# A decoder layer on one core: prompt compression moved under the GLA normalisation, sample constants made earlier, and another order of branches and page loads for the last four samples

## The reference

```python
def compress(kv, w1, b1, w2, pe):            # prompt and samples, keys and values alike
    ...
    first = jnp.einsum('bnpgd,pdh->bngh', ch + pe[:CMP_STRIDE, None, :], w1r[:CMP_STRIDE])
    second = jnp.einsum('bnpgd,pdh->bngh', ch + pe[CMP_STRIDE:, None, :], w1r[CMP_STRIDE:])
    hid = jax.nn.gelu(first[:, :-1] + second[:, 1:] + b1)
    return jnp.einsum('bngh,hd->bngd', hid, w2)

o_gla = rmsnorm(o_gla.astype(x.dtype), gla_norm_g) * jax.nn.silu(...)      # the normalisation
o_nsa = gates[:, :, 0] * o_cmp + gates[:, :, 1] * o_slc + gates[:, :, 2] * o_win
```

## Time and profile before

| | |
|---|---|
| median of 3 runs | 2411.33 us (2409.88 to 2413.12) |
| the profiled execution | 2411.11 us, its span 2409.5 us |
| busy in the span | PE 2166.9 us (90%), PEld 1748.8 (73%), DVE 883.5 (37%), ACT 435.9 (18%), POOL 487.8 (20%) |
| mean granted clock of TensorE | 0.953 of full speed |
| GLA | 429 to 545 us |
| compression | 546 to 582 us |
| samples | 582 to 700 us |
| prompt's attention | from 700 us |

### The profile page before, as it was taken

The page is one execution under the profiler, slowest core; times in us unless marked ns, Lnnn a source line. Parts: engine busy times, 40 slices in busy tenths (PEclk is TensorE's granted clock), DMA queues, the critical chain, the costliest instruction groups (busy, mean ns, idle before and its releaser), DMA issues. The chain is left out here.

```text
span 2409.5 us, 30785 instructions
## 1 busy us (share of the span) xinstructions
PE 2166.9 (90%) x11874; PEld 1748.8 (73%) x11874; DVE 883.5 (37%) x1520; ACT 435.9 (18%) x897; POOL 487.8 (20%) x425
## 2 busy tenths in 40 slices
PE   3789999887669888999999998799999999999994
PEld 3678888666346555788888665588888888888883
DVE  1443122662236656521121114622232222534336
ACT  0241000331125555200000012311111000000001
POOL 2112210003011111522121122622322223000002
PEclk9899999895879999999999999899999999999997
DMA  8432112636320000101211210311111111122421
GB/s 238 118 94 80 38 35 65 175 81 166 103 73 1 1 1 1 36 25 45 48 31 44 81 35 27 107 35 50 37 35 52 35 52 35 48 87 93 151 79 72
DMA packets 236729, 157.32 MB, mean 65 GB/s; under 512 B 33926, under 2 KB 229032, under 8 KB 236561
## 3 DMA queue, kind: packets, MB, share of 16 engines
q1 hardware_dynamic: 224758, 139.93, 20.6%
q0 software_dynamic: 2960, 13.73, 1.6%
q10 hardware_dynamic: 8906, 2.24, 0.5%
HBM read 143.33 MB, written 16.71 MB: 66 GB/s over the span
## 5 line engine op out<-in xcount | busy, mean ns | idle before, releaser
L207 PE MATMUL ps<-hT,ring 128*128 128x264 f32 x2144 | 495.7, 389 | 18.7 <-DVEq L2925 14.8
L207 PE MATMUL ps<-big,ring 128*128 128x264 f32 (+1 forms) x2080 | 503.2, 400 | 4.5 <-DVEq L2763 4.5
L207 PEld LDWEIGHTS ps<-hT,ring 128*128 128x128 f32 x2144 | 410.1, 192 | 91.3 <-DVEq L2925 14.9
L207 PEld LDWEIGHTS ps<-big,ring 128*128 128x128 f32 x2080 | 395.9, 190 | 101.4 <-DVEq L2763 4.9
L3130 PE MATMUL ps<-big,ring 128*128 128x264 f32 x1056 | 240.7, 388 | 2.5 <-PEq L3317 2.5
L3130 PEld LDWEIGHTS ps<-big,ring 128*128 128x128 f32 x1056 | 201.7, 191 | 37.7 <-issue 2.9
L207 PE MATMUL ps<-big 128*128 128x264 f32 x608 | 138.5, 386 | 0.2 <-DVE big L2505 0.2
L207 PEld LDWEIGHTS ps<-big 128*128 128x128 f32 x608 | 115.4, 190 | 20.3 <-issue 0.6
L2510 DVE TENSOR_TENSOR big<-big,ps 128x528 f32<-128x528 f32 x70 | 49.3, 704 | 184.8 <-PE ps L207 177.9
L946 DVE TENSOR_TENSOR big<-big,ps 128x528 f32<-128x528 f32 x63 | 44.2, 703 | 163.7 <-PE ps L207 163.3
L2980 POOL TENSOR_TENSOR ring<-ring 128x512 f32<-128x512 f32 x22 | 30.0, 1365 | 366.1 <-DMA ring<-in_w_ff_up 364.0
(11 more groups left out here) (452 smaller groups left out, 2578.9 us busy)
## 6 DMA issues: line engine op xcount, KB each, us to landing
ring<-in_w_ada SPq DMA_DIRECT2D x44, 512.0 KB, 5.7
ring<-in_w_in SPq DMA_DIRECT2D x34, 512.0 KB, 5.1
ring<-in_w_ff_down SPq DMA_DIRECT2D x16, 1024.0 KB, 5.0
ring<-in_w_ff_gate SPq DMA_DIRECT2D x22, 512.0 KB, 4.0
ring<-in_w_ff_up SPq DMA_DIRECT2D x22, 512.0 KB, 5.2
big<-in_cache_slc_kv SPq DMA_DIRECT2D x48, 128.0 KB, 2.1
ring<-in_w_ff_down SPq DMA_DIRECT2D x8, 768.0 KB, 4.3
x_kept<-big SPq DMA_DIRECT2D x8, 528.0 KB, 7.6
```

Of the source, the lines that this page charges most:

```text
L207: ins = pe.matmul(out, w[:, k, :], rhs(k), start=first and k == 0, stop=last and k == nk - 1)
```

## The change

Four parts. **First**, the sums of the compression are moved into the end of GLA: six steps ahead of each transposed tile, the rest after the last. For it GpSimd lays out keys and values there, once scores and sums of the prompt have been made, and zeroes and SyncE loads the value's first layer in three pieces into buffers that have come free. **Second**, SyncE loads the pages of the first two samples in GLA, those of the third and fourth in the compression (GpSimd no longer loads any), and there too four units of modulation and the window keys of the first two samples. **Third**, the samples' constants are made in the compression beside the gelu; the gates are spread by products with columns of the identity, broadcast to 64, in place of `sel`. **Fourth**, the last four samples take the window branch before the pages. Their page loads are split into a key and a value half, each with its page number read again: the key halves of a sample once its keys of the first round have been turned, the value halves after the first four's page values have been summed.

```diff
+def load_first_layer_piece(sp, w, piece, g, done):
+    t0, to = piece
+    r = slice(64 * g, 64 * g + 64)
+    sp.dma_start(to[r, :, r], w[0].rearrange("(t d) h -> d t h", d=HD)[:, t0:t0 + to.shape[1], :]).then_inc(done, 16)
...
@@ stage_gla, SyncE
+                    for n, piece in enumerate(w1v):
+                        sp.wait_ge(w1v_zero, 2 * n + 2)
+                        for g in range(2):
+                            load_first_layer_piece(sp, I["cmp_w1_v"], piece, g, w1v_in)
+                    sp.wait_ge(m_done, 9)
+                    for j in range(NPAGE):
+                        load_page(sp, m, I, "cache_slc_kv", 0, j, m.past[0][:, j, :], m.past_in[0])
+                    sp.wait_ge(o_mm, 2 * QT)
+                    sp.wait_ge(ei_ok, 2)
+                    for j in range(NPAGE):
+                        load_page(sp, m, I, "cache_slc_kv", 1, j, m.past[1][:, j, :], m.past_in[1])
                 sp.wait_ge(s0_done, 2 * p + 2)
...
@@ stage_gla, GpSimd
+            pool.wait_ge(kv_mm, 4 * QT)
+            pool.wait_ge(s0_out[0], 16)
+            pool.wait_ge(kl_T, 2)
+            for n, (t0, to) in enumerate(w1v):
+                for g in range(2):
+                    pool.memset(to[64 * g:64 * g + 64, :, 64 - 64 * g:128 - 64 * g], 0.0).then_inc(w1v_zero, 1)
+                pool.wait_ge(w1v_zero, 2 * n + 2)
+            pool.wait_ge(a_mm, 2 * QT)
+            pool.tensor_copy(kt[0].rearrange("p t n -> p n t"),
+                             m.zT[:, Z_KC, 0:SEQ].rearrange("p (n t) -> p n t", t=CS)).then_inc(kt_done, 1)
+            pool.wait_ge(kt_done, 1)
+            pool.wait_ge(o_mm, 2 * QT)
+            pool.tensor_copy(kt[1].rearrange("p t n -> p n t"),
+                             m.zT[:, Z_VC, 0:SEQ].rearrange("p (n t) -> p n t", t=CS)).then_inc(kt_done, 1)
...
@@ stage_gla, TensorE
+            def compress_sums(n):
+                for _, x in zip(range(n), todo):
+                    kv, t = divmod(x, CL)
+                    if t == 0:
+                        pe.wait_ge(kt_done, kv + 1)
+                        pe.wait_ge(w1v_in if kv else w1_in, 96 if kv else 32)
+                    ins = pe.matmul(cmp_ps[kv], weight[x], kt[kv][:, t % CS, t // CS:t // CS + 63], start=t == 0,
+                                    stop=t == CL - 1)
+                    if t == CL - 1:
+                        ins.then_inc(m.cmp_mm, 1)
+
+            pe.wait_ge(smp_kept, 2)
             for i in range(TT):
                 n = P if i < QT else ST
+                compress_sums(6)
                 pe.wait_ge(scaled, i + 1)
...
+            compress_sums(2 * CL)
...
@@ stage_compress, SyncE
+            sp.wait_ge(m.cmp_mm, 1)
+            for s in range(2):
+                load_ada_unit(sp, m, I, FIRST_LATE + s, s, m.ada_first[s])
+            for b in range(2, 4):
                 for j in range(NPAGE):
                     load_page(sp, m, I, "cache_slc_kv", b, j, m.past[b][:, j, :], m.past_in[b])
+            for b in range(2):
+                sp.dma_start(kw[b], win[:, b, :, 0:GD]).then_inc(m.first_keys[b], 16)
+            for s in range(2, 4):
+                load_ada_unit(sp, m, I, FIRST_LATE + s, s, m.ada_first[s])
...
@@ stage_compress, TensorE
+            for k in range(3):
+                for hd in range(HP):
+                    col = (k * HP + hd) * ST
+                    for g in range(2):
+                        one = 8 * k + HP * g + hd
+                        ins = pe.matmul(ps[64 * g:64 * g + 64, 0, col:col + ST],
+                                        m.ident[0:24, one:one + 1].to_broadcast([24, HD]), m.gnT[:, :], start=True,
+                                        stop=True)
...
@@ stage_samples
-    seq = [(q, br) for q in range(NQ) for br in range(3)]
+    seq = [(0, 0), (0, 1), (0, 2), (1, 0), (1, 2), (1, 1)]
...
@@ stage_samples, SyncE
+            def half_pages(b, part, done):
+                for j in range(NPAGE):
+                    page = sp.value_load(m.pt[0:1, bass.ds((BQ + b) * NPAGE + j, 1)], min_val=0, max_val=m.n_pool - 1)
+                    rows = src[bass.ds(page, 1)][:, :, part].rearrange("o t c -> t (o c)")
+                    sp.dma_start(kv[b][:, j, part], rows).then_inc(done[b], 16)
+
+            def window_keys(n):
+                sp.dma_start(kw[n % 2], win[:, n, :, 0:GD]).then_inc(k_in[n % 2], 16)
+
+            for b in range(BQ):
+                sp.dma_start(vw[:, b], win[:, b, :, GD:2 * GD]).then_inc(v_in, 16)
+            for b in range(BQ):
+                sp.wait_ge(kT, b + 1)
+                half_pages(b, slice(0, GD), keys_in[1])
+            for b in range(2, BQ):
+                sp.wait_ge(kT, kn(0, 2, b) - 1)
+                window_keys(b)
+            sp.wait_ge(pv, 2)
+            for b in range(BQ):
+                half_pages(b, slice(GD, 2 * GD), values_in[1])
+            sp.wait_ge(pv, 3)
+            for b in range(BQ):
+                if b < 2:
+                    window_keys(BQ + b)
+                sp.dma_start(vw[:, b], win[:, BQ + b, :, GD:2 * GD]).then_inc(v_in, 16)
+            for b in range(2, BQ):
+                sp.wait_ge(kT, kn(1, 2, b) - 1)
+                window_keys(BQ + b)
```

More of the change, by code:

```diff
@@ L1111, in _ @@
             sp.wait_ge(st_out, 32)
-            sp.wait_ge(s0_out, 32)
-            sp.wait_ge(w1_in, 32)
+            for p in range(2):
+                sp.wait_ge(s0_out[p], 16)
             sp.wait_ge(values_out, 64)
@@ L1550, in _ @@
+            ins.then_inc(gates_mm, 1)
             for kv in range(2):
@@ L1568, in _ @@
[L1568 to L1576 removed]
+            steps = [0]
@@ new lines, in chain, with compressed @@
+            def chain(ins):
+                steps[0] += 1
+                ins.then_inc(c_own, 1)
+                dve.wait_ge(c_own, steps[0])
+            def compressed(kv):
+                gelu_dve(dve, x[kv], u[kv], h[kv], kv, g_act, g_dve)
+            compressed(0)
+            dve.wait_ge(c_pool, 9)
+            for g in range(2):
+                for hd in range(HP):
+                    r = slice(64 * g, 64 * g + 64)
+                    dve.tensor_scalar(c.Qb[r, :, g, hd, :], m.zT[r, Z_Q + hd, SEQ:T].rearrange("p (b t) -> p b t", t=DS),
+                                      HD ** -0.5, None, ALU.mult)
@@ L1763, in _ @@
                     pe.wait_ge(v_in, 16 * BQ * (q + 1))
+                if br == 1 and q:
+                    for b in range(BQ):
+                        pe.wait_ge(values_in[q][b], 16 * NPAGE)
                 if br == 0:
```

219 lines of the change are left out of this document (97 added, 122 removed).

## The result

Over 20 runs of each kernel on the same chips the median went from 2411.45 us to **2421.6 us**, slower by 10 us. The ratio of the two samples is 1.0052, with a 95% interval of 1.0041 to 1.0064 (the medians alone give 1.0042). The median hides a second fact: the 20 runs lie in two groups, 12 between 2414.3 and 2422.3 us (median 2419.6) and 8 between 2428.1 and 2438.5 us (median 2433.5), with nothing between 2422.4 and 2428. The kernel before has one group, 2408.8 to 2417.8. These are not disturbed runs; the experiments show where the second group comes from. The profiled execution (2431.57 us, span 2430.0) belongs to the upper group, so what follows is the upper group's picture until e3 and e9 show the lower one.

What follows compares the result with a forecast made beforehand. TensorE, VectorE and ScalarE in turn were taken to set the end. First sample score 15.8 us earlier, sample stage 23.1 us longer: +7.3 on 2411.11 us, 2418.4, given as 2419; range 2411 to 2437.

Steps and rivals of the forecast that it cites:

- Part 1: End of GLA: 128 sum records at 0.112 us each, full clock, layouts hidden on GpSimd; compression begins at 555.7.
- A: Sums in GLA: the clock stays at 1.00 under them; main case, total 2414 to 2426, chance 0.42.
- case B: Sums in GLA: the clock falls to half, first sample score at 592.9, total 2433.7; chance 0.30.
- rival E: Sums in GLA wait over 8 us for GpSimd's copies or late value weights, 2427 and more; chance 0.08.
- Part 2: Compression: SyncE's 16 page issues at 1.137 us set a 22.0 us stage; first sample score 15.8 us earlier.
- Part 3: Sample stage: 64 half-page issues at 1.137 us delay window keys; last branch ends 23.1 us later.
- both waits: Sample stage: TensorE waits for window keys 13 to 17 us in the third branch, about 17 in the fifth.
- Rival C: Sample stage: half-page issues of at most 0.70 us bring window keys in time, 2386, down to 2379; chance 0.07.

Runs made afterwards that it cites:

- e3: Changed kernel with TensorE's two pauses before the transposes filled by identity products: 2421.3 us, ratio 1.0031, seven runs in one group.
- e9: Changed kernel with SyncE reading a sample's eight page numbers in one go before issuing its half pages: 2424.0 us, ratio 1.0035, two groups.
- e4: Changed kernel with eight of the compression's 16 SyncE pages issued by GpSimd: 2424.7 us, ratio 1.0052.
- e11: Changed kernel with the first six sums made later, so TensorE's two pauses become one: 2436.8 us, ratio 1.0105.
- e1: Changed kernel with the last four samples' half pages loaded from fixed page numbers, none read from the table: 2386.75 us, ratio 0.989.
- e2: Changed kernel with the sample stage's whole-page loads and branch order put back as before: 2406.8 us, ratio 0.9963.
- e5: Changed kernel with the same SyncE loads reordered, window keys no longer behind 32 half-page issues: 2408.4 us, ratio 0.9962, two groups.
- e10: e7 without its fillers, all else the same: 2393.9 us, ratio 0.993.
- e7: Changed kernel with e3's fillers, e4's GpSimd pages, and half the sample stage's half pages issued by GpSimd: 2378.6 us, ratio 0.986.

## Why the prediction was right, and where it was not

The forecast was 2419, slower, with a range of 2411 to 2437; measured were 2421.6, and all 20 runs of the sample but the highest, 2438.5, lie in the range. Its steps:

**Part 1.** The cost of a record held: with the full clock six sums and four transposes take 1.72 us (e3) where I had 1.94, the 0.2 for waits being the error. From G to F I had 43.9 us (577.8 - 533.9) in the main case, A, and e9 has 43.2; in case B 59.0 (592.9 - 533.9), and the changed kernel's profiled execution has 57.3. GpSimd's layouts, with which I bounded a danger, took 1.97 and 1.98 us and kept nobody waiting, so rival E is out.

**Part 2.** VectorE was done 12.7 us before SyncE's last issue, which is what I had named as the sign. T0 to F is 22.5, predicted 22.1. e4 takes pages from SyncE and the stage follows.

**Part 3.** The place and the cause of both waits were as predicted. The 13.8 us of the first was how much later than before the keys would come, F+47.8 against F+34.05; they came at F+47.0, 12.9 later. As a wait of TensorE my numbers (wanted at F+31) made it 16.8, and it was 13.4, since TensorE reached it only at F+33.6. The second was predicted at 16.6 and was 15.0. The branch ends are F+61.0 predicted and F+61.1 measured for the third, F+102.6 and F+101.0 for the fifth, F+125.6 and F+123.9 for the last. That the third fits to 0.1 us is in part luck: the keys came 0.8 us early, and the rest of the branch took 3.0 us longer than before (14.1 against 11.1), where I had 2. From F to A the forecast comes to 130.1 (107.0 + 23.1); the four profiled executions with this sample stage (after, e3, e4, e11) have 128.3 to 132.9. The price, which I had only from whole pages, was 1.115 against 1.137. What the profile of before did not show, namely of what that price is made, e1 and e9 do: 0.64 us for the number and its use, of which the read is 0.57, and 0.47 for the issue from a fixed address.

**Rival C** was wrong in its condition. With an issue at 0.47 us, under its bound of 0.70, it gave 2386, and e1, where that condition holds, measured 2386.75. Its mechanism is borne out, the waits nearly go, but the term is not: it had F to A shorter by 9.3 us than before, and e1's one trace, of the upper kind, has 103.0 against 107.0. How the four faster runs come to 2386 no trace shows.

**Rival B and the chances.** Here lies the error. I had put A and B as two mechanisms of which one would be true of the kernel, with 0.42 and 0.30. Both are true of it, each of some runs: the lower group's 2419.6 is A's 2418.6, the upper group's 2433.5 is B's 2433.7. The step that failed is the one that set the 2.93 us gap, after which the clock had fallen, against "a start at full clock": it asked whether the clock falls, not whether it falls in every run. Of the changed kernel's runs 8 in 20 were of kind B, and of the seven profiled executions that had the two short pauses six (after, e1, e2, e4, e5, e10) show the sums at half clock and one (e9) at full. The median of 20 came out close to A because slightly more than half of the runs were A; with the sort of draw that e2 or e4 had it would have been near 2433. So the forecast's number owes part of its accuracy to that draw.

The Trainium skill (TensorE: Matmul & The Clock Gate, Part 4) has transposes not bringing the full clock. I gave that rule no weight on account of the earlier trace rows; in the upper group every tile has four transposes and the clock stays at 0.50 for 29.8 us, which fits the rule. I read the earlier trace rows too strongly: from 593.6 to 599.6, just before that stretch, TensorE had been busy for 3.8 us, for the most part with products that are no transposes. A purer stretch stands in the same trace, at the end of GLA. TensorE makes nothing but transposes there, the 16 from 536.86 to 540.3 of the earlier trace rows, and is then idle for 1.44 us; the clock falls to 0.50 under them and is 1.00 again from 541:

```profile
538.00:540.00 2.00, 2.00 (x11) 1.88 (x9) 1.97 (x4) 1.46 (x3) 0.00 (x0) 0.50 0.00 0
540.80:544.20 3.40, 2.48 (x17) 1.76 (x18) 3.26 (x6) 1.99 (x4) 0.00 (x0) 1.00 0.54 154
```

So in this kernel the full clock did come back with transposes as TensorE's only work, and it did not come back where 63-column sums took most of the time (27 us before, 29.8 after). What in the sums makes the difference, no run here tests. The same page's advice of continuous work (Why this matters for your kernels), which I had said the trace did not bear out, is half true here: it keeps the full clock (e3), but does not win it back (e11).

**What is open.** Why one run falls and the next does not, at the same pauses. That e2, e4 and e10 had 16 of 17 runs in the upper group and the changed kernel 8 of 20 may be chance, the chip or a small shift of the code; no run tells these apart. The two pauses are the same in all seven traces (0.51 to 0.52 and 0.86 to 0.87 us), and of the kernels run on one chip e1 had 2 of 6 runs in the upper group and e2 and e4 together 10 of 11, so the chip alone does not explain it. e5 and e9 had 6 of 10 each. The groups of the runs without a trace are told by their times alone. Nor is it settled why F to A differs by up to 4.6 us between executions of the same sample stage (128.3 us at a clock of 0.69 in the changed kernel, 132.9 at 0.68 in e3, 129.4 at 0.72 in e4).

## What to carry to other kernels

Before a load is split or moved ahead, count issues and not bytes: multiply them by the interval from one issue to the next in the same queue, and ask which small load, needed sooner, stands behind them. If the price is in reading an address, let a second, idle engine issue half, or put the urgent load first; here the other order alone made 2408.4 of 2421.6 us (e5), and the sharing, with e3 and e4, 2378.6.

When work is moved onto TensorE next to a short pause, price it at both clocks and expect runs of both kinds; the few products that close the pause cost about 0.4 us here (G to T0 in e3 and e9) and save 13.9 in each run that would have fallen.

When a kernel's times fall in two groups, compare an experiment group by group: e4 looked 3 us worse in the median, and its stage was 6.6 us shorter.

## What the runs showed of the hardware

- **A pause of 0.5 and one of 0.9 us, close together, can cost the clock for the next 30 us.** TensorE was busy in 29.8 of 29.8 us of 63-column sums and transposes at 0.50, and the clock did not come back; where it had not fallen, the same work stayed at 1.00 for 16 us (e3, e9). In these traces the clock falls within 4 us of G or not at all before the sums are done. A fall costs 13.9 us here (2433.5 - 2419.6).
- **A page number read from memory costs SyncE about 0.6 us, and reads don't overlap** (0.64 with its use as the address in e1, 0.57 for the read in e9); GpSimd's interval of 1.15 us for such a page is the same as SyncE's. The issue from a fixed address is 0.47. The Trainium skill (DMA: Bandwidth & Descriptors, Issuing engines are not separate DMA queues) says that issuing from several engines saves only the sequencer's time, usually small beside the transfer. The trace agrees with the first half and not with the second: 64 issues at 1.115 are 71 us of sequencer time in a stage of 128, and the other order alone took 23 us out of it (e5), the sharing, with the window keys behind 16 issues instead of 32, 31 us (e7).
- **Half a page costs as much to issue as a whole one**: 32 whole pages go out in 34.87 us in e2, 32 halves in 34.91 in the changed kernel.
